# State-space constants and angles computed through PSUM, spread over pairs 2 to 9 of the first feed-forward stage, and three more pairs of it by seven products

## What is computed

```python
for layer in range(DEPTH):                       # DEPTH = 2
    h = h + 0.5 * swiglu(rmsnorm(h, ffn1_norm[layer]), ...)   # stages 0 and 2
    hn = rmsnorm(h, mix_norm[layer])
    # layer 0: GLA and S5 mixers; layer 1: sparse attention
    h = h + mix
    h = h + cross_attn(rmsnorm(h, xa_norm[layer]), mem_n, ...)
    h = h + 0.5 * swiglu(rmsnorm(h, ffn2_norm[layer]), ...)   # stages 1 and 3

def swiglu(h, w_gate, w_up, w_down):             # 1024 -> 2816 -> 1024
    return (silu(h @ w_gate) * (h @ w_up)) @ w_down

# S5: constants from lambda and log_dt, (32 groups x 64 states = 128 x 16 numbers)
dt = exp(log_dt);  mag = exp(lr * dt)
ab_re = mag * cos(li * dt);  ab_im = mag * sin(li * dt)
den = lr * lr + li * li;  f_re, f_im = (ab - 1) / lambda
```

## Time and profile before

| what | value |
|---|---|
| median of the three runs | 2129.93 us |
| the profiled execution: its own time | 2133.41 us |
| the profiled execution: span on the core | 2131.3 us |
| granted TensorE clock, mean | 0.998 of full speed |
| PE busy | 2113.0 us, 99% |
| DVE busy | 1337.0 us, 63% |
| ACT busy | 792.1 us, 37% |
| POOL busy | 1548.8 us, 73% |

### The profile page before, as it was taken

One profiled execution on the slowest core, in us unless ns is written; L12 is line 12 of the kernel. 1 busy time (PEld: TensorE's weight loads), 2 busy tenths in 40 slices (PEclk: granted clock), 3 DMA queues, 4 the chain that ended last, 5 costly groups with the idle time before them and its releaser, 6 DMA issues. The chain is left out here.

```text
span 2131.3 us, 35973 instructions
## 1 busy us (share of the span) xinstructions
PE 2113.0 (99%) x12886; PEld 1853.7 (87%) x12886; DVE 1337.0 (63%) x1942; ACT 792.1 (37%) x1506; POOL 1548.8 (73%) x1398
## 2 busy tenths in 40 slices
PE   9999999999999999999999999999999999999998
PEld 7879988888888899998889998886878888999987
DVE  6986797595545476664386777356882546677533
ACT  5115412125223345541255552134362234555312
POOL 7767898567883778888768787785767556788874
PEclk9999999999999999999999999999999999999999
DMA  6333333223431233334323333332323212333332
GB/s 198 98 119 106 103 99 120 82 93 95 119 110 49 91 108 105 110 101 122 98 87 113 105 110 99 98 99 78 106 85 94 79 60 84 116 103 113 101 99 79
DMA packets 115412, 214.98 MB, mean 101 GB/s; under 512 B 12832, under 2 KB 14400, under 8 KB 115008
## 3 DMA queue, kind: packets, MB, share of 16 engines
q1 hardware_dynamic: 111024, 202.03, 30.7%
q10 hardware_dynamic: 4240, 10.99, 1.5%
HBM read 208.77 MB, written 4.19 MB: 100 GB/s over the span
## 5 line engine op out<-in xcount | busy, mean ns | idle before, releaser
L525 POOL TENSOR_TENSOR w_split<-w_raw,w_split 128x512 fp32r<-128x512 f32 (+1 forms) x502 | 691.9, 1378 | 42.7 <-ACT w_split L1791 1.2
L601 PE MATMUL ps<-x,w_split 128*128 128x512 f32 (+1 forms) x1830 | 707.5, 387 | 4.1 <-DVE arena L2196 2.7
L603 PE MATMUL ps<-x,w_split 128*128 128x512 f32 (+1 forms) x1830 | 698.9, 382 | 0.0
L602 PE MATMUL ps<-x,w_split 128*128 128x512 f32 (+1 forms) x1830 | 698.7, 382 | 0.0
L515 POOL TENSOR_SCALAR w_split<-w_raw 128x512 fp32r<-128x512 f32 x498 | 344.1, 691 | 368.7 <-PE ps L603 351.1
L810 PE MATMUL ps<-x,w_split 128*128 128x264 f32 (+1 forms) x1792 | 504.1, 281 | 4.4 <-issue 2.2
L812 PE MATMUL ps<-x,w_split 128*128 128x264 f32 (+1 forms) x1792 | 503.6, 281 | 0.0
L811 PE MATMUL ps<-x,w_split 128*128 128x264 f32 (+1 forms) x1792 | 502.0, 280 | 0.0
L601 PEld LDWEIGHTS ps<-x,w_split 128*128 128x128 f32 x1830 | 343.9, 188 | 82.5 <-issue 10.5
L603 PEld LDWEIGHTS ps<-x,w_split 128*128 128x128 f32 x1830 | 343.9, 188 | 67.2
L602 PEld LDWEIGHTS ps<-x,w_split 128*128 128x128 f32 x1830 | 344.0, 188 | 66.8 <-issue 1.4
(11 more groups left out here) (342 smaller groups left out, 2488.6 us busy)
## 6 DMA issues: line engine op xcount, KB each, us to landing
w_raw<-in_stream SPq DMA_DIRECT2D x758, 256.0 KB, 2.8
arena<-in_memT ACTq DMA_DIRECT2D x2, 1024.0 KB, 5.9
s_tables<-kv ACTq DMA_DIRECT2D x4, 512.0 KB, 3.0
arena<-s_tables ACTq DMA_DIRECT2D x4, 512.0 KB, 4.7
out<-h ACTq DMA_DIRECT2D x6, 256.0 KB, 2.6
h<-in_xT SPq DMA_DIRECT2D x4, 256.0 KB, 4.9
h<-in_xT SPq DMA_DIRECT2D x2, 512.0 KB, 6.2
w_raw<-in_stream SPq DMA_DIRECT2D x5, 128.0 KB, 5.1
```

The lines of the kernel that those rows point to most:

```text
L525: pool.tensor_tensor(lo, x, hi.bitcast(F32), ALU.subtract).then_inc(split_ready if half else S("half_split"), 1)
L601: pe.matmul(dst, wh, xh, start=start, stop=False)
L602: pe.matmul(dst, wh, xl, start=False, stop=False)
L603: return pe.matmul(dst, wl, xh, start=False, stop=stop)
```

## The change

Four edits.

1. `SEVEN[0]` goes from 14 to 11: pairs 11, 12 and 13 of stage 0 are taken by seven products.
2. The S5 constants keep most scratch in PSUM bank 0 (`scratch`), `turns` keeps its running value in PSUM bank 1 in place of SBUF. A step then mostly has at most one operand in SBUF to read. The powers of lambda have a copy in PSUM; this adds three copies, 108 steps in place of 105.
3. The asides move: constants in six parts at pairs 2, 3, 5, 6, 7, 9; turns at 5 to 8; ACT's tables one pair behind their turns, at 6 to 9; the token sums S4 and S3 at pairs 2 and 3.
4. In stage 2 the memory split stands behind hidden chunks 4 to 11 on DVE and ACT, no longer ahead of chunk 4.

```diff
-CONSTANTS_AT, TABLES_AT = [2, 3, 5, 6, 7], 8
+CONSTANTS_AT, TABLES_AT = [2, 3, 5, 6, 7, 9], 5
-SEVEN = {0: 14, 1: 3, 2: 4, 3: 3}
+SEVEN = {0: 11, 1: 3, 2: 4, 3: 3}
-SUMS_AT = {1: "S2", 5: "S4", 6: "S3"}
+SUMS_AT = {1: "S2", 2: "S4", 3: "S3"}
+SCRATCH_BANK, TURN_BANK = 0, 1
...
-        tiny = sb("tiny", [P, 12, 16])
+        tiny = sb("tiny", [P, 4, 16])
+        scratch = ps[:, SCRATCH_BANK, 0:17 * 16].rearrange("p (i n) -> p i n", n=16)
...
                 else:
-                    with act.Fori(1, 5) as i:
+                    with act.Fori(1, 3 if f == 2 else 5) as i:
                         for s in range(4):
                             part(bass.ds(i * 4 + s, 1), s, i * 4 + (dn + s - 3))
+                    if f == 2:
+                        memory_split(1)
+                        with act.Fori(3, 5) as i:
+                            for s in range(4):
+                                part(bass.ds(i * 4 + s, 1), s, i * 4 + (dn + s - 3))
...
-                    if f == 0 and TABLES_AT <= p < TABLES_AT + 4:
-                        table(p - TABLES_AT)
+                    if f == 0 and TABLES_AT < p <= TABLES_AT + 4:
+                        table(p - TABLES_AT - 1)
...
-                k, r, p = tn(9), tn(10), tn(11)
+                r, k, p = tiny[:, 2, :], scratch[:, 4, :], scratch[:, 5, :]
...
+                def copied(at):
+
+                    return scratch[:, 11 + at:13 + at, :]
...
+                for at in range(L_POW, L_POW + 6, 2):
+                    if at:
+                        times(at, at - 2, L_POW)
+                    chain(dve.tensor_copy(copied(at), powers[:, at:at + 2, :]))
+                yield
...
-                chain(dve.tensor_tensor(a, time, ph, ALU.mult))
-                chain(dve.tensor_scalar(b, a, MAGIC, MAGIC, ALU.add, ALU.subtract))
-                chain(dve.tensor_tensor(a, a, b, ALU.subtract))
+                x = ps[:, TURN_BANK, :].rearrange("p (j k) -> p j k", j=4)
+                chain(dve.tensor_tensor(x, time, ph, ALU.mult))
+                chain(dve.tensor_scalar(b, x, MAGIC, MAGIC, ALU.add, ALU.subtract))
+                chain(dve.tensor_tensor(x, x, b, ALU.subtract))
...
-            ffn(2, lambda: (memory(1), memory_split(1)))
+            ffn(2, lambda: memory(1))
```

More of the change, by code:

```diff
@@ L730, in project @@
                 for t in range(4 + 4 * full, nt):
-                    tile(at + t, ((at + t) % 2, BANKS[t % 4]), x, (free_sem, free_base + t - 3))
+                    need = free_base + (t // 2 - 1 if per == 2 else t - 3)
+                    tile(at + t, ((at + t) % 2, BANKS[t % 4]), x, (free_sem, need))
             def ffn(f):
@@ L1799, in s5_constants @@
                 act.wait_ge(S("th_ready"), 1)
[L1800 to L1801 removed]
+                act.activation(scratch[:, 1, :], scratch[:, 0, :], ACT.Abs).then_inc(S("th_abs"), 1)
+                act.activation(scratch[:, 3, :], scratch[:, 0, :], ACT.Sin).then_inc(S("th_trig"), 1)
                 act.wait_ge(S("th_abs"), 1)
[L1803 removed]
+                act.activation(scratch[:, 2, :], scratch[:, 1, :], ACT.Sin, scale=-1.0, bias=epsc[:, 1:2]
                                ).then_inc(S("th_trig"), 1)
@@ L2039, in _ @@
             norm(4)
-            ffn(2, lambda: memory_split(1))
+            ffn(2)
             norm(5)
@@ L2235, in ffn @@
                 else:
-                    with dve.Fori(1, 5) as i:
+                    with dve.Fori(1, 3 if f == 2 else 5) as i:
                         for s in range(4):
                             part(bass.ds(i * 4 + s, 1), s, i * 4 + (base + s + 1))
+                    if f == 2:
+                        memory_split(1)
+                        with dve.Fori(3, 5) as i:
+                            for s in range(4):
+                                part(bass.ds(i * 4 + s, 1), s, i * 4 + (base + s + 1))
                 for d in (20, 21):
@@ L2454, in s5_constants @@
             def s5_constants():
-                lr, dt, th, ab_r, ab_i = tn(0), tn(1), tn(2), tn(3), tn(4)
+                lr, th, t = (tiny[:, i, :] for i in (0, 1, 3))
+                angle, cos, sin, turn, dt, ab_r, ab_i, den, t1 = (scratch[:, i, :] for i in (0, 2, 3, 4, 6, 7, 8, 9, 10))
                 mag, ph, pl = sc5[:, C_MAG:C_MAG + 16], sc5[:, C_PH:C_PH + 16], sc5[:, C_PL:C_PL + 16]
@@ L2468, in s5_constants @@
                 chain(dve.tensor_tensor(th, li, dt, ALU.mult))
[L2469 to L2475, removed]
+                reduce_angle(th, t1)
+                chain(dve.tensor_scalar(angle, th, PI_BELOW, -PI_BELOW, ALU.min, ALU.max))
+                chain(dve.tensor_scalar(turn, th, 0.15915494309189535, None, ALU.mult))
+                chain(dve.tensor_scalar(t1, turn, 4096.0, MAGIC, ALU.mult, ALU.add))
+                chain(dve.tensor_scalar(ph, t1, MAGIC, 1.0 / 4096, ALU.subtract, ALU.mult))
+                dve.tensor_tensor(pl, turn, ph, ALU.subtract).then_inc(S("th_ready"), 1)
+                dve.wait_ge(S("th_ready"), 1)
                 yield
                 dve.wait_ge(S("th_trig"), 2)
-                chain(dve.tensor_tensor(l_r, tn(7), mag, ALU.mult))
-                chain(dve.tensor_tensor(l_i, tn(8), mag, ALU.mult))
+                chain(dve.tensor_tensor(l_r, cos, mag, ALU.mult))
+                chain(dve.tensor_tensor(l_i, sin, mag, ALU.mult))
                 chain(dve.tensor_copy(ab_i, l_i))
                 chain(dve.tensor_scalar(ab_r, l_r, 1.0, None, ALU.subtract))
-                den, t1 = tn(5), tn(6)
                 chain(dve.tensor_tensor(den, lr, lr, ALU.mult))
-                chain(dve.tensor_tensor(t1, li, li, ALU.mult))
-                chain(dve.tensor_tensor(den, den, t1, ALU.add))
+                chain(dve.tensor_tensor(t, li, li, ALU.mult))
+                chain(dve.tensor_tensor(den, den, t, ALU.add))
                 chain(dve.reciprocal(den, den))
@@ L2497, in s5_constants @@
                 chain(dve.tensor_tensor(mag, mag, mag, ALU.mult))
+                def copied(at):
+                    return scratch[:, 11 + at:13 + at, :]
                 def times(dst, x, y):
[L2501 to L2510, removed]
+                    xr, xi, yr, yi = powers[:, x, :], powers[:, x + 1, :], copied(y)[:, 0, :], copied(y)[:, 1, :]
+                    dr, di = powers[:, dst, :], powers[:, dst + 1, :]
+                    chain(dve.tensor_tensor(t1, xi, yi, ALU.mult))
+                    chain(dve.tensor_tensor(dr, xr, yr, ALU.mult))
+                    chain(dve.tensor_tensor(dr, dr, t1, ALU.subtract))
+                    chain(dve.tensor_tensor(t1, xi, yr, ALU.mult))
+                    chain(dve.tensor_tensor(di, xr, yi, ALU.mult))
+                    chain(dve.tensor_tensor(di, di, t1, ALU.add))
+                for at in range(L_POW, L_POW + 6, 2):
[3 more added lines that the diff above has]
+                yield
                 for m in range(1, STRIDE):
```

8 lines of the change are left out of this document (3 added, 5 removed).

## The result

The changed kernel takes 2118.7 us (median of four runs, 2117.99 to 2119.5) where the kernel before takes 2129.53 in the same series (2128.87 to 2130.78): a ratio of 0.9944, 95% interval 0.9932 to 0.9956. Measured once more among the experiments, with the kernel before at 2129.95, it took 2119.87, a ratio of 0.9951 (0.9938 to 0.9965).

What follows compares the result with a forecast made beforehand. PE, busy 99%, was taken as the bound. Stage 0's -7.1 us (fewer columns and less waiting) and stage 2's -0.9 gave -8.0, from a median of 2129.9 to 2121.9 us, range 2119.5 to 2126.5.

Steps and rivals of the forecast that it cites:

- What bounds the kernel: Whole kernel: PE, busy 99% of 2131.3 us, so only fewer matmul columns or less waiting on PE shorten it.
- rival 1: Stage 0: DVE early, PE the bound, T1 at 124.6 with a 4.7 us lead; 2119.7 us, chance 0.22.
- The cause of the waits: Stage 0: loses 7.4 us on PE, all because DVE is late, its steps with two SBUF operands lengthened beside POOL.
- What a lead is worth: First seven-product pair of stage 0: T1 at 127.0 leads by 2.3 us, so 3.0 us are lost.
- The price: Entry to the seven-product pairs: about 0.9 us lost for each us of missing lead, counted from T1's start.
- The ledger of DVE: Stage 0, gate(2) to T1 of pair 11: DVE's work sums to 81.4 us, so T1 starts at about 127.
- the seven exceptions: Constants: seven of 108 small steps keep both operands in SBUF or copy SBUF to SBUF; 2.5 us for holds.
- Stage 2: Memory split moved from ahead of chunk 4 to behind chunk 11 removes PE's wait: -0.9 us.
- The fewer columns: Stage 0: three pairs go from 10.89 to 10.00 us each by seven products: -2.7 us.
- The rule that speaks against it: Skill page's fixed 120 cycles for PSUM reads against 58 from SBUF: 65 ns more per step, forecast about 2130.7.
- rival 2: DVE's small steps in PSUM cost 0.07 us more each, T1 at 136.5; 2131.4 us, chance 0.09.
- Rival 3: PSUM operands don't free DVE from POOL, the hold being on the whole engine; T1 at 149.0, 2144 us, chance 0.04.

Runs made afterwards that it cites:

- PSUM alone: Changed kernel with SEVEN[0] at 14 and asides, tables, token sums and stage 2's split in their old places, scratch and turns in PSUM: 2123.47 us, ratio 0.9968.
- the order alone: Changed kernel with scratch and turns back in SBUF and SEVEN[0] at 14, new order kept: 2133.98 us, ratio 1.0015.
- 10 steps more: Changed kernel with ten extra 16-column copies into PSUM at the end of the constants' sixth part, right ahead of T1: 2121.30 us, ratio 0.9957.
- the turns in SBUF: Changed kernel with only the turns' running value back in SBUF, constants' scratch still in PSUM: 2127.76 us, ratio 0.9983.
- both in SBUF: Changed kernel with constants' scratch and turns' running value back in SBUF, order and SEVEN[0] = 11 kept: 2139.07 us, ratio 1.0039.
- twenty steps more: Changed kernel with twenty extra 16-column copies into PSUM right ahead of T1: 2124.03 us, ratio 0.9972.

## Why the prediction was wrong in size

- **What bounds the kernel** held. PE's own starts give the whole result: 10.2 us in stage 0 and 1.3 in stage 2 are 11.5, where the medians show 10.8 and 10.1. The way it went is rival 1, "DVE is early, PE is the bound", 2119.7, which had a chance of 0.22.
- **The cause of the waits** held: held steps of DVE. PSUM alone brings stage 0's pairs 8.2 us forward, the order alone 3.2 back.
- **The step that failed is "What a lead is worth", with the T1 it was given: 3.0 us lost at the entry, measured -0.1 in its own count (109.9 us for eleven pairs of 10.0).** It has two parts, which 10 steps more tells apart.
  1. The price, 1.2 us. With T1 at 126.89, where the forecast had it, the eleven pairs took 111.84 us: 1.8 lost and not 3.0. The price was drawn through two points, stage 1's lead of 4.75 with 0.8 lost and stage 0's 1.57 with 3.7 lost, and the lead was counted from the start of T1. In both points T1 was itself held by POOL: it took 1.73 and 1.79 us, where the free one takes 0.70. Counted from T1's end they are 3.0 and -0.2 us ahead, and they lie on the line of the table. The slope of the forecast was about right (0.9 for 1.0). What it left out is that a T1 which is free, or nearly (0.70 in 10 steps more, 0.95 in the changed kernel), gives about a us more of lead for the same start.
  2. The ledger of DVE, 2.0 us. It said 81.4 us from gate(2) to T1, and 79.7 were measured, from a start 0.3 earlier. From 10 steps more to the changed kernel T1 starts 1.95 us earlier, and the stretch is 1.97 shorter. By its items: the 108 steps took 23.5 us where 23.8 and 2.5 for held ones were set; the turns 21.1 for 21.6; S4 and S3 6.9 for 7.0; the memory norm 8.1 for 8.1; the eight gates 20.2 for 18.4, since their product was still held (1100 ns on average). The part of the sum that the change made new was right within 0.2 us per turn and 0.01 us per step; I had set too much for the seven exceptions and too little for the gates.
- **Stage 2** was 0.9 in the forecast and is 1.2: the listed wait leaves out 0.28 us of restart.
- **The fewer columns** were right: 2.7 forecast, 2.5 measured between the medians of the changed kernel and the one with SEVEN[0] at 14.
- The terms then give 2129.9 - 8.0 - 3.1 - 0.3 = 2118.5, and 2118.7 was measured. That the two are so close is in part luck: T1 of stages 1 and 3 alone moves an execution by 1 us each.
- **The range** should have reached the case in which both engines meet. I had placed T1's floor at 124.6 and given this case 0.22, then ended the range at 2119.5, 0.2 under it, with no room for the terms of stage 2 and of the price.
- **The rule that speaks against it.** The Trainium skill, "VectorE: DVE Perf Modes", section "The TRN2 errata", has 120 cycles fixed for a read from PSUM and 58 from SBUF, by estimate 65 ns more. In the changed kernel's trace a step of 16 columns that multiplies or adds in PSUM takes 182 ns, and an unheld one in SBUF took 174 to 176 in the trace of before. The traces disagree; rival 2 is out.
- **Rival 3**, a hold on the whole engine, is out: in ten kernels of this study that keep the turns' value in PSUM, the 20 steps of each that read it took 0.69 or 0.70 us, all 200.

## What to carry to other kernels

Before a chain on an engine is called slow, look whether its steps of one form have one length: where they vary between a floor and a multiple of it, another engine holds them, and changing where the operands lie can be worth more than moving the work. Price a missing lead from the end of the step that is waited for, ask whether that step was held in the rows that the price comes from, and look for the point from which a lead is worth nothing more. And a wait in the list costs PE more than its listed length; read the starts around it, and the granted clock behind it.

## What the runs showed of the hardware that was not expected

**One SBUF input is enough to be held, if the output is in SBUF too.** The forecast put the hold on the second SBUF operand, though it counted copies from SBUF to SBUF among its seven exceptions. The trace of before had shown more, in a row of its groups that the prediction didn't read; the line has one input:

```profile
L2448 DVE TENSOR_SCALAR tiny<-tiny 128x16 f32<-128x16 f32 x12 | 4.4, 363 | 0.4
```

Its mean is as long as the 361 ns of the two-input L2447 beside it. With the turns in SBUF the roundings L2552 and L2556 have one input. Two cases, from the timeline of DVE with both in SBUF:

```profile
95.14 1.40 DVE L2556 TENSOR_SCALAR kv<-kv 128x512 f32<-128x512 f32 x1
...
133.70 0.43 DVE L2556 TENSOR_SCALAR kv<-kv 128x512 f32<-128x512 f32 x1
```

Free it takes 0.43 us, and only 6 of 24 such steps in three kernels did; the others took 0.73 to 1.40. In PSUM the same step takes 0.69, always. Their mean is 0.83. So PSUM makes this step slower when nobody disturbs and faster on average. The 12 small steps L2458, also with one input, had a mean of 482 ns in SBUF, above the two-input L2457's 280. The Trainium skill, "SBUF — State Buffer", section "SBUF: two separate sides", says this: POOL and DVE share one pair of ports, which a DVE instruction needs with two SBUF inputs or in a mode that reads through both ports, and whoever starts first keeps it to the end. The traces agree: the one-input step is faster with both its operands in SBUF (0.43 us for 0.69) and only then held, and in stages 1 and 3 a start 0.01 us ahead of POOL decided.

**A step that reads two SBUF operands and writes to PSUM is held as well.** In the kernel with PSUM alone the first step of every turns was held, four times for the same time; a group of DVE's from 45 to 154 us:

```profile
L2543 DVE TENSOR_TENSOR ps<-arena,sc 128x512 f32<-128x512 f32 x4 | 7.1, 1782 | 0.0
```

In the changed kernel the same step (L2551) took 0.69 to 0.70 in all four cases, since POOL was idle when it started. So an output in PSUM doesn't free a step with two SBUF inputs. It does free one with a single SBUF input: in the nine kernels with the constants in PSUM the small steps of the forms `ps<-tiny`, `ps<-powers` and `ps<-vec` with one input never took over 179 ns.

**A restart of PE isn't free, and a long wait can cost its clock.** The wait of 0.90 us cost 1.18. The one of 5.35 us cost 5.8 by the starts: 130.57 to 136.59 is 6.02 us, where two matmuls of 264 columns are 0.23 apart; and there the granted clock was 0.50 (1.2 GHz) already, so the matmuls behind it started 0.22 us apart until it came back to 1.00 (2.4 GHz) at 144.6. The length of one wait alone doesn't tell: behind 2.73 us in the kernel before the clock stayed at 1.00, and with twenty steps more it fell behind waits of 1.09 and 1.84. The runs here give no rule for it.
